# A two-layer token model on one core: the block layer of the second attention moved between its projections, its softmax beside the first attention units

## What is computed

```python
def compress(t, pe, w1, w2):            # 31 windows of 32 positions, step 16
    blk = kvh(t)[:, cidx] + pe[:, None, :]
    hid = gelu(einsum('bnlgd,ldc->bngc', blk, w1))   # 2048 -> 256
    return einsum('bngc,cd->bngd', hid, w2)          # 256 -> 64
k_cmp = rms_norm_2(compress(kc, pe_k, c1k, c2k), k_gain[0])
v_cmp = compress(vc, pe_v, c1v, c2v)
...
s_c = einsum('bqghd,bngd->bgqhn', qb, k_cmp) * scale + bias
p_c = masked_softmax(s_c, cmp_end <= t)
o_c = einsum('bgqhn,bngd->bqghd', p_c, v_cmp)
...
out = gb[..., 0:1] * o_c + gb[..., 1:2] * o_s + gb[..., 2:3] * o_w
```

## Time and profile before

| | us |
|---|---|
| median of 3 runs (2533.8 to 2537.71) | 2536.79 |
| the profiled execution | 2534.55 |
| its span | 2532.8 |
| PE busy | 2333.9 (92%) |
| DVE, ACT, POOL busy | 1077.1, 679.9, 1216.0 |

### The profile page before, as it was taken

The page is one execution under the profiler, slowest core; times in us unless marked ns, Lnnn a source line. Parts: engine busy times, 40 slices in busy tenths (PEclk is TensorE's granted clock), DMA queues, the critical chain, the costliest instruction groups (busy, mean ns, idle before and its releaser), DMA issues.

```text
span 2532.8 us, 41596 instructions
## 1 busy us (share of the span) xinstructions
PE 2333.9 (92%) x16684; PEld 1708.9 (67%) x16684; DVE 1077.1 (43%) x1674; ACT 679.9 (27%) x1255; POOL 1216.0 (48%) x690
## 2 busy tenths in 40 slices
PE   4999998899999799978869976998999999899999
PEld 1445776688878444468856555657887787688877
DVE  5976752555500445653341344665224421422200
ACT  2125112333300224333322113772002231323300
POOL 1007886588877000000015511557787325688876
PEclk8999999999999899989989986999999999999999
...
DMA packets 59343, 211.74 MB, mean 84 GB/s; under 512 B 6720, under 2 KB 7752, under 8 KB 59200
## 3 DMA queue, kind: packets, MB, share of 16 engines
...
...
## 4 chain that ended last, share of the span: by engine, by line
PE 63%; POOL 18%; issue 12%; DVE 4%; DMA 1%; ACT 1%; POOLq 0%; ACTq 0%; DVEq 0%; SPq 0%
PE banks L368 15%; PE banks L424 9%; POOL WH L404 9%; PE banks L425 9%; PE banks L426 9%; POOL WL_A L407 8%; PE banks L1423 4%; PE banks L1465 3%; PE banks L561 2%; PE banks L593 2%; PE banks L574 2%; DMA W<-stream 1%; PE banks L876 1%; PE banks L1874 1%; PE banks L466 1%
## 5 line engine op out<-in xcount | busy, mean ns | idle before, releaser
L404 POOL TENSOR_TENSOR WH<-W,ZERO 128x1024 fp32r<-128x1024 f32 x240 | 464.1, 1934 | 677.0 <-PE banks L426 365.7
L407 POOL TENSOR_TENSOR WL_A<-W,WH 128x1024 fp32r<-128x1024 f32 x164 | 419.9, 2561 | 12.9
L368 PE MATMUL banks<-H,W 128*128 128x512 f32 x752 | 332.7, 602 | 21.6 <-ACT H L735 16.6
L424 PE MATMUL banks<-HF,WH 128*128 128x512 f32 x704 | 276.3, 392 | 15.5 <-DVE HF L518 7.8
L368 PEld LDWEIGHTS banks<-H,W 128*128 128x128 f32 x752 | 144.4, 193 | 208.6 <-issue 205.7
L425 PE MATMUL banks<-HF,WH 128*128 128x512 f32 x704 | 275.0, 391 | 0.0
L426 PE MATMUL banks<-HF,WL_A 128*128 128x512 f32 x704 | 274.9, 390 | 0.0
L425 PE MATMUL banks<-HR,WH 128*128 128x512 f32 x416 | 166.6, 400 | 0.0
L424 PEld LDWEIGHTS banks<-HF,WH 128*128 128x128 f32 x704 | 132.7, 189 | 48.0 <-issue 15.7
L426 PEld LDWEIGHTS banks<-HF,WL_A 128*128 128x128 f32 x704 | 132.9, 189 | 27.8
L425 PEld LDWEIGHTS banks<-HF,WH 128*128 128x128 f32 x704 | 133.0, 189 | 26.8
(11 more groups left out here) (407 smaller groups left out, 4556.3 us busy)
## 6 DMA issues: line engine op xcount, KB each, us to landing
...
```

Source lines behind the costliest of these rows:

```text
L368: last = nc.tensor.matmul(bank, W[:, slot, (lo + k) * P:(lo + k + 1) * P], r, start=(k == 0), stop=(k == len(rhs) - 1))
L404: nc.gpsimd.tensor_tensor(WH[:, half, :], W[:, slot, :], ZERO[:, 0:1].to_broadcast([P, D]), ALU.add)\
L407: nc.gpsimd.tensor_tensor(WL[stage][half], W[:, slot, :], WH[:, half, :], ALU.subtract)\
L424: nc.tensor.matmul(out_ap, w_hi, hi, start=start, stop=False)
```

## The change

- **Stages.** `cmp_k`, `cmp`, `nturn` and `cmp_p` are gone, and `nsa` runs into `attend2` without a barrier. The eight units of the first layer stand in the ring behind projection units 4 to 7 and 10 to 13, and SP's loads of this stretch are written out.
- **Order of the projections.** Compressed keys and values come first (`TILE`), then the other keys and values, then the queries. The small work is placed by half units (`beside`, 40 steps) and the projections use three banks in place of four.
- **First layer.** PE reads the step-16 views of `SH` itself. The position part is a matmul of one column with the same weights (`pe_first_layer`) into two more columns of the bank, which ACT uses as the bias of its gelu. Four matmuls with zeros open the bank. The second layer and the key norm stand at later steps.
- **Bias table and score tiles.** POOL loads `BIAS2` in two parts between its splits (after units 13 and 17) and fills the score tiles with NEG behind its last split, in place of DVE.
- **Block softmax.** Its steps stand behind the units 0, 1, 2, 4 and 5 of DVE's attention, the exponentials in ACT's, the scaling on POOL behind units 5 and 6, the transposes on PE at steps 8 to 11. The output banks of the first two pairs start from zeros, and their block products are added at units 12 and 15 (`LATE_BLOCKS`).

```diff
...
+TILE = (8, 9, 10, 11, 12, 13, 16, 17, 0, 1, 2, 3, 4, 5, 6, 7, 14, 15, 18, 19)
+NSA_RING = {NSA_AT[u]: TILE[u] for u in range(NSA_UNITS)}
+NSA_RING.update({NSA_AT[u] + 1: NSA_UNITS + 4 * k + q for u, (k, q) in FIRST_LAYER.items()})
...
+        def split_nsa(pool, first, last):
+
+            u0 = U0["nsa"]
+            for u in range(first, last):
+                at = u0 + NSA_AT[u]
+                slot, half = at % W_SLOTS, u % S_SLOTS
+                pool.wait_ge(w_full[slot], 16 * (at // W_SLOTS + 1))
+                if u >= S_SLOTS:
+                    pool.wait_ge(unit_done, u0 + NSA_AT[u - S_SLOTS] + 1)
+                nc.gpsimd.tensor_tensor(WH[:, half, :], W[:, slot, :], ZERO[:, 0:1].to_broadcast([P, D]), ALU.add)\
+                    .then_inc(s_split, 1)
+                pool.wait_ge(s_split, 2 * (SPLIT0["nsa"] + u) + 1)
+                nc.gpsimd.tensor_tensor(WL["nsa"][half], W[:, slot, :], WH[:, half, :], ALU.subtract)\
+                    .then_inc(s_split, 1)
+
...
                             pe.wait_ge(p_max, 2 * (a0 + i - 2) + c + 1)
+                        elif blocks is not None:
+                            pe.wait_ge(b_dve, 8 * (i + 1))
                         nc.tensor.matmul(psum[2 * (i % 2) + c][:, 0:u["nk"]], u["q"][c], u["k"][c], start=True,
                                          stop=True).then_inc(p_sc, 1)
                 if i == 1 and first is not None:
...
                     j = i - SUM
                     u = units[j]
@@ -582,10 +602,22 @@
                         if u["pair"] >= 2:
                             for done in p_out:
                                 pe.wait_ge(done, BASE_OUT[stage] + u["pair"] - 1)
-                        if blocks is not None:
+                        if blocks is not None and u["pair"] < 2:
+                            if u["pair"]:
+                                pe.wait_ge(b_act, 6)
+                            for c in range(2):
+                                nc.tensor.matmul(bank[DH * c:DH * (c + 1), :], con("ident", lo=0, hi=32)[:, DH:2 * DH],
+                                                 con("scan", lo=0, hi=32), start=True, stop=False)
+                        elif blocks is not None:
                             for c in range(2):
                                 v, p = blocks(u["pair"], c)
                                 nc.tensor.matmul(bank[DH * c:DH * (c + 1), :], v, p, start=True, stop=False)
+                    if blocks is not None and j in LATE_BLOCKS:
+                        pe.wait_ge(v_c, 4 + 4)
+                        for c in range(2):
+                            v, p = blocks(LATE_BLOCKS[j], c)
+                            nc.tensor.matmul(psum[6 + LATE_BLOCKS[j]][DH * c:DH * (c + 1), :], v, p, start=False,
+                                             stop=(LATE_BLOCKS[j] != u["pair"]))
                     for copied in p_pt:
                         pe.wait_ge(copied, a0 + j + 1)
                     for b in range(u["nk"] // P):
@@ -593,12 +625,15 @@
                             last = nc.tensor.matmul(bank[DH * c:DH * (c + 1), u["cols"]], u["v"][c][b],
                                                     PT[stage][j % 2][c][:, b * P:(b + 1) * P],
                                                     start=(blocks is None and b == 0),
-                                                    stop=(b == u["nk"] // P - 1 and (blocks is None or u["last"])))
+                                                    stop=(b == u["nk"] // P - 1
+                                                          and (blocks is None or u["last"] and u["pair"] > 0)))
                     last.then_inc(p_pv, 1)
...
...
+        def pe_values2(pe):
+            pe.wait_ge(s_ev, BASE["nsa"].ev + NSA_UNITS)
+            pe.wait_ge(v_c, 4 + 4)
+            pe.wait_ge(m_app, 12)
+            pe.wait_ge(e_root, DT + 1)
+            pe.wait_ge(m_root, 3)
+            for t in range(4):
+                for j in range(4):
+                    last = nc.tensor.transpose(psum[4 + t][:, j * P:(j + 1) * P],
+                                               (VS, VS, VW, VW)[j][:, j % 2, t * P:(t + 1) * P], con("ident"))
+                last.then_inc(v_tr, 1)
+
...
+        def pe_block_scores(pe):
+            pe.wait_ge(e_kk, DT + 1)
+            pe.wait_ge(s_gelu, BASE["nsa"].gelu + 4)
+            for c in range(2):
+                for qi in range(S // P):
                     for p in range(2):
                         for hg in range(HG):
                             lo = DH * c
@@ -876,31 +947,13 @@
                             last = nc.tensor.matmul(
                                 psum[2 * c + qi // 2][:, at:at + N_CMP], QN[lo:lo + DH, HG * p + hg, qi * P:(qi + 1) * P],
                                 KCN[lo:lo + DH, (2 * p + c) * N_CMP:(2 * p + c + 1) * N_CMP], start=True, stop=True)
-            last.then_inc(b_pe, 1)
+                last.then_inc(b_pe, 1)
+
...
+                        nc.vector.tensor_tensor(CP[c][:, qi, HG * p:HG * (p + 1), 0:n], scores[:, HG * p:HG * (p + 1), 0:n],
+                                                BIAS2[:, h:h + HG, cols], ALU.add).then_inc(b_dve, 1)
+
+        def dve_block_step(dve, i):
+            V = nc.vector
+            if i == 0:
+                for c in range(2):
+                    dve.wait_ge(b_dve, 8 * (c + 1))
+                    V.tensor_reduce(some(0, c), flat(c), AX_X, ALU.max, negate=True).then_inc(b_dve, 1)
+            elif i == 1:
+                for c in range(2):
+                    dve.wait_ge(b_dve, 17 + c)
+                    V.tensor_scalar(some(0, c), some(0, c), -0.01 * NEG, None, ALU.min).then_inc(b_low, 1)
+            if 1 <= i < 3:
+                c = i - 1
                 dve.wait_ge(b_low, 1 + c)
-                V.tensor_tensor(flat[c], flat[c], wide(0, c), ALU.add).then_inc(b_dve, 1)
-            for c in range(2):
+                V.tensor_tensor(flat(c), flat(c), wide(0, c), ALU.add).then_inc(b_dve, 1)
+            if 4 <= i < 6:
+                c = i - 4
                 dve.wait_ge(b_act, c + 1)
-                V.tensor_reduce(some(1, c), flat[c], AX_X, ALU.add).then_inc(b_dve, 1)
-            for c in range(2):
-                dve.wait_ge(b_dve, 23 + c)
-                V.tensor_scalar(some(1, c), some(1, c), 0.5, None, ALU.max).then_inc(b_dve, 1)
-            for c in range(2):
-                dve.wait_ge(b_dve, 25 + c)
-                V.reciprocal(some(0, c), some(1, c)).then_inc(b_dve, 1)
-            for c in range(2):
-                dve.wait_ge(b_dve, 27 + c)
-                for p in range(2):
-                    h = 2 * HG * p + HG * c
-                    rec = some(0, c).rearrange("p (q h) -> p q h", q=4)[:, :, HG * p:HG * (p + 1)]
-                    f = some(1, c).rearrange("p (q h) -> p q h", q=4)[:, :, HG * p:HG * (p + 1)]
-                    last = V.tensor_tensor(f, rec, GT[:, :, 3 * h:3 * (h + HG):3], ALU.mult)
-                last.then_inc(b_dve, 1)
...
-
+                V.tensor_reduce(some(1, c), flat(c), AX_X, ALU.add).then_inc(b_dve, 1)
+            if i == 5:
+                for c in range(2):
+                    dve.wait_ge(b_dve, 21 + c)
+                    V.tensor_scalar(some(1, c), some(1, c), 0.5, None, ALU.max).then_inc(b_dve, 1)
+                for c in range(2):
+                    dve.wait_ge(b_dve, 23 + c)
+                    V.reciprocal(some(0, c), some(1, c)).then_inc(b_dve, 1)
+                for c in range(2):
+                    dve.wait_ge(b_dve, 25 + c)
+                    for p in range(2):
+                        h = 2 * HG * p + HG * c
+                        rec = some(0, c).rearrange("p (q h) -> p q h", q=4)[:, :, HG * p:HG * (p + 1)]
+                        f = some(1, c).rearrange("p (q h) -> p q h", q=4)[:, :, HG * p:HG * (p + 1)]
+                        last = V.tensor_tensor(f, rec, GT[:, :, 3 * h:3 * (h + HG):3], ALU.mult)
+                    last.then_inc(b_dve, 1)
+
+        def act_block_probs(act, c):
+            act.wait_ge(b_dve, 19 + c)
+            nc.scalar.activation(CP[c], CP[c], ACT.Exp).then_inc(b_act, 1)
+
+        def pool_block_scale(pool, c):
+            pool.wait_ge(b_dve, 27 + c)
+            nc.gpsimd.tensor_tensor(flat(c), flat(c), wide(1, c), ALU.mult).then_inc(b_nrm, 1)
+
+        def pe_block_turn(pe, g):
+            c, p = g // 2, g % 2
+            pe.wait_ge(b_nrm, c + 1)
+            if g:
+                pe.wait_ge(b_act, 2 + g)
+            for qi in range(S // P):
+                src = CP[c][:, qi, HG * p:HG * (p + 1), :].rearrange("p a b -> p (a b)")
+                last = nc.tensor.transpose(psum[7][:, qi * P:(qi + 1) * P], src, con("ident"))
+            last.then_inc(b_pe, 1)
+
+        def act_block_copy(act, g):
+            act.wait_ge(b_pe, 3 + g)
+            nc.scalar.activation(PCT[2 * (g % 2) + g // 2], psum[7][:, :], ACT.Copy).then_inc(b_act, 1)
 
...
+        def pe_first_layer(pe, kind, q):
+
```

(32 more changed lines are left out.)

487 lines of the change are left out of this document (227 added, 260 removed).

## The result

The change made the kernel slower: 2555.89 us median (2553.7 to 2559.18) against 2537.25 for the kernel before in the same comparison, a ratio of 1.0071 with a 95% interval of 1.0053 to 1.009. The forecast was 2519 with a range of 2505 to 2537. The sign was wrong, and the time lies outside the range.

The account below looks back on a forecast made before the run. PE was taken as the bound, so gaps in its work are span. Replacing 85.8 us by 53.6, less 0.5 for a root wait and 15.9 in the attention, gained 15.8 us: 2534.55 to 2519, range 2505 to 2537.

Parts of the forecast that it names:

- Wide first-layer instructions: First compression layer on PE: 128 instructions with 124 columns at 0.115 us each, 14.7 us, nothing added for strided reads.
- the rival's 0.103 us: First layer on PE: strided columns cost double, 0.103 us more per wide instruction, 13.2 us, kernel 2532; chance 0.12.
- One-column instructions: First layer's position part on PE: 128 new instructions at 0.11 us each, 14.1 us, ends 10.9 and 14.7.
- The 48-column row: Trace row of a small 48-column projection, about 0.11 us per instruction, used to price one-column instructions.
- The slower rival: Eight first-layer groups between projection units: one-column groups cost the clock, 3.5 us each, up to 28 us, 2547; chance 0.08.
- The four spreads: Key-norm spreads on PE, now between projection units: 2.1 us, as before.
- Block scores: 128 PE instructions before the attention: 60 in 5 us at full clock, 68 at 0.168 us; 16.4 us, ends 10.9 and 21.7.
- Wait of 1.0 us: Before the value transposes: PE waits for DVE's last apply, 0.73 us, 1.0 with hand-over, covered by nothing.
- The square root's 0.5 us: Projections: the fifth tile's variance waits for a square root that ACT can start only half a unit before; 0.5 us.
- Rivals of both signs: Block scores: a rival held 2.4 GHz throughout, 5.5 us less, 2513, chance 0.13; the slow end was 21.7 us, as before.
- The attention: Added attention time: bias additions 1.5, softmax 8, table load 1.3, PE work 4.1, hand-over 1; together 15.9 us.
- the softmax term: First six attention units: the block softmax on DVE delays PE by 8 us, ends 1 and 11.

## Why the prediction was wrong

Between first projection matmul and first attention score the forecast missed 45.7 us. Two steps of the prediction failed above all: it took the strided read on PE at nothing, and it took the granted clock as 1.00 around the first-layer groups. The terms, in the order of its own sum:

- **Wide first-layer instructions, 0.115 us.** Wrong: 0.217 strided. DVE's strided read was taken as a sign that the stride is cheap, and the value at the bottom of the bounds was chosen; the other bound, a doubling, was close (0.217 / 0.118 = 1.84), and the rival's 0.103 us more per instruction was measured as 0.10. The chance of 0.12 was too small for a question with no row on PE. The Trainium skill, page Advanced Engine Details and Errata, section Memory Cachelines, spoke for the penalty, and these runs agree with it.
- **One-column instructions, 0.11 us.** Right: 0.107. The 48-column row was a good neighbour. With both, a group took 5.04 us, not 3.6: 8 × 1.44 = **11.5 us**.
- **The clock.** The forecast had the clock at 1.00 around the groups; behind them it fell, and the stretch lost 29.8 − 5.2 = **24.6 us** to it that the projections before did not. That is more than the whole forecast gain of 15.8 us and as much as the 24.4 us between the two spans: without it the change would have been no loss, but with the other terms no gain either. The slower rival named the place, the eight groups and a price of 28 us, but gave it 0.08, and argued "against it: a group is shorter than the 5 us that the clock held in the earlier trace rows". That was worked out with the unstrided price, 3.5 us. With the stride the group is 5.04 us long, though length alone, as the doubled groups show, does not lose the clock. The two rivals were treated as nearly independent, 0.12 and 0.08; the experiments show that they act together, since neither the strided reads nor the one-column matmuls alone cost any clock.
- **The four spreads, 2.1 us, "as before".** Wrong: the earlier trace rows show 8 instructions in 2.10 us because they ran side by side. Standing alone they take 1.05 us each, and four of those in the units lost their partner too: **6.4 us**.
- **Block scores, 16.4 us.** 21.3 us. The clock started at 1.00 and held for about 5 us, as forecast. What was wrong are the prices per instruction, 0.085 and 0.168 us, both from the mean in the earlier trace rows: that order has seven switches between the halves of the rows, each of which runs some instructions together. The change's order has one switch, and its instructions take 0.111 and 0.214 us. The miss is **4.9 us**; with the order of before the scores take 17.7 us in place of 21.7, so the order explains 4.0 of it.
- Wait of 1.0 us, no wait for weights or POOL: right, at this pace; in the faster versions PE did wait 0.9 to 1.0 us for POOL. The square root's 0.5 us did not show. The transposes took 1.9 us, as forecast.

Rivals of both signs spoke of the clock in the scores; it fell within them in every run with 64 rows. Together 11.5 + 24.6 + 6.4 + 4.9 = 47.4 us, against 45.7 to be explained; the 1.7 us too many were not found. The attention was forecast at 15.9 and took 12.8. The direction and the mechanism (DVE late in the first units, so that PE waits) are right, the softmax term is 5.7 instead of 8. That the sum came so near is partly luck: it had no term for the lower clock at the attention's start.

So the idea of the change was sound: with the blocks packed by DVE the same move gives a ratio of 0.9945, with the scores on all rows 0.9858 and with alternating halves 0.9875. The strided reads together with the one-column matmuls, and the clock that the two cost, turned it into a loss.
